# A decoder layer on one core: the first 128 tokens go ahead through attention output, output projection and queries, and VectorE weights three of the last v rows

## The reference

```python
y_a = a_pre @ w_conv_out
y_b = attn_o @ w_attn_out
mix = jax.nn.sigmoid(g_a) * y_a + jax.nn.sigmoid(g_b) * y_b
x = x + gate1[:, None, :] * (mix @ w_out)
h2 = _modulate(_rmsnorm(x, norm2_w), shift2, scale2)
y = _peer(h2.reshape(-1, D_MODEL), peer_w_q, peer_sub_keys, peer_u, peer_v).reshape(x.shape)
return x + gate2[:, None, :] * y
```

```python
act = jax.nn.gelu(jnp.einsum('thkd,td->thk', u_tab[e], hb).astype(jnp.float32))
return jnp.einsum('thk,thkd->td', (g * act).astype(hb.dtype), v_tab[e])
```

## Time and profile before

| | us |
|---|---|
| median of 3 runs (1149.05 to 1152.76) | 1151.59 |
| the profiled execution | 1151.69 |
| its span, first to last instruction | 1149.9 |
| TensorE busy | 983.1 |
| VectorE busy | 718.0 |
| POOL busy (asking) | 575.2 |
| ScalarE busy | 242.6 |

### The profile page before, as it was taken

The page is one execution under the profiler, slowest core; times in us unless marked ns, Lnnn a source line. Parts: engine busy times, 40 slices in busy tenths (PEclk is TensorE's granted clock), DMA queues, the critical chain, the costliest instruction groups (busy, mean ns, idle before and its releaser), DMA issues.

```text
span 1149.9 us, 10850 instructions
## 1 busy us (share of the span) xinstructions
PE 983.1 (85%) x3401; PEld 497.9 (43%) x3401; DVE 718.0 (62%) x1765; ACT 242.6 (21%) x593; POOL 575.2 (50%) x618
## 2 busy tenths in 40 slices
PE   6998889999999999998777777777777777778888
PEld 3456766667677874542232222222222222222333
DVE  2357466888644798768567467477576576444342
ACT  2111223113402133341112112121121021121111
POOL 0201001002000567777777777777777777777760
PEclk9999889999999999999999999999999999999999
DMA  9961423779537699999999999999999999999994
GB/s 314 351 221 57 152 74 129 256 256 286 148 120 287 245 345 382 409 408 410 409 409 409 409 410 409 409 409 410 410 409 409 410 409 410 409 410 409 409 411 179
DMA packets 123403, 379.89 MB, mean 330 GB/s; under 512 B 11612, under 2 KB 21080, under 8 KB 123348
## 3 DMA queue, kind: packets, MB, share of 16 engines
q0 software_dynamic: 86208, 312.92, 69.3%
q1 hardware_dynamic: 36966, 66.19, 16.7%
q10 hardware_dynamic: 174, 0.11, 0.1%
HBM read 377.59 MB, written 1.59 MB: 330 GB/s over the span
## 4 chain that ended last, share of the span: by engine, by line
PE 37%; DMA 28%; POOL 20%; issue 8%; DVE 6%; ACT 1%; SPq 0%; DVEq 0%; ACTq 0%; POOLq 0%
DMA big<-peer_v,oT 13%; POOL big L1060 9%; POOL big L1049 8%; PE twoA L567 7%; DMA big<-peer_u,oT 7%; PE twoA L880 5%; DMA r<-peer_u,oT 4%; PE twoD L935 4%; PE twoD L937 3%; PE twoD L821 3%; PE twoA L545 2%; POOL r L1049 2%; PE twoA L490 2%; PE twoD L809 1%; DMA big<-w_in 1%
## 5 line engine op out<-in xcount | busy, mean ns | idle before, releaser
L1049 POOL DMA_INDIRECT big<-peer_u,oT x230 | 216.5, 941 | 179.1 <-DVEq L1777 107.0
L1060 POOL DMA_INDIRECT big<-peer_v,oT x266 | 252.6, 950 | 87.5 <-issue 69.6
L1819 DVE CUSTOM_DVE_ANT_0 big<-big,twoA 128x1024 f32<-128x1024 f32 x128 | 156.2, 1221 | 143.5 <-DMA big<-peer_u,oT 142.5
L1819 DVE CUSTOM_DVE_ANT_0 big<-big,twoD 128x1024 f32<-128x1024 f32 x102 | 123.3, 1218 | 54.9 <-DMA big<-peer_u,oT 53.6
L935 PE MATMUL twoD<-big 128*128 128x512 f32 x176 | 97.0, 633 | 40.4 <-DMA big<-peer_v,oT 38.7
L567 PE MATMUL twoA<-hT,big 128*128 128x288 f32 x448 | 117.6, 419 | 0.0
L935 PE MATMUL twoD<-big,modT 128*128 128x512 f32 x132 | 73.1, 636 | 31.1 <-DMA big<-peer_v,oT 30.7
L567 PEld LDWEIGHTS twoA<-hT,big 128*128 128x128 f32 x448 | 86.2, 196 | 28.8 <-issue 5.9
L937 PE MATMUL twoD<-big 128*128 128x512 f32 x176 | 89.9, 592 | 0.0
L935 PEld LDWEIGHTS twoD<-big 128*128 128x128 f32 x176 | 27.5, 188 | 104.6 <-DMA big<-peer_v,oT 96.4
L935 PE MATMUL twoD<-big,rstd 128*128 128x512 f32 x90 | 49.9, 636 | 21.8 <-DMA big<-peer_v,oT 21.7
(11 more groups left out here) (368 smaller groups left out, 1419.0 us busy)
## 6 DMA issues: line engine op xcount, KB each, us to landing
big<-w_ada SPq DMA_DIRECT2D x12, 2048.0 KB, 8.3
big<-w_in SPq DMA_DIRECT2D x5, 2048.0 KB, 13.6
big<-w_in SPq DMA_DIRECT2D x9, 1024.0 KB, 7.6
big<-peer_w_q SPq DMA_DIRECT2D x3, 2048.0 KB, 8.8
big<-peer_v,oT POOLq DMA_INDIRECT x266, 18.5
big<-w_out SPq DMA_DIRECT2D x2, 2048.0 KB, 11.7
big<-peer_u,oT POOLq DMA_INDIRECT x230, 16.3
big<-w_conv_out SPq DMA_DIRECT2D x1, 2048.0 KB, 13.7
```

The source lines that it names most:

```text
L1049: pool.indirect_dma_start(urows[i % NU], None, peer_u, bass.IndirectOffsetOnAxis(ap=eidx[:, t, s:s + 1], axis=0)).then_inc(u_in[i % NU], 16)
L1060: pool.indirect_dma_start(vrows[j % NV], None, peer_v, bass.IndirectOffsetOnAxis(ap=eidx[:, t, s:s + 1], axis=0)).then_inc(v_in[j % NV], 16)
L1819: dve.tensor_tensor_reduce(out=urows[i % NU], in0=urows[i % NU], in1=h2tok[t][:, :], scale=1.0, scalar=0.0, op0=ALU.mult, op1=ALU.add, acc ...
```

## The change

`attnout`, `out`, residual, norm and the first eight query blocks are done in two passes: columns 0 to 127 (tile 0, whose attention is long finished) and columns 128 to 287 (REST, 160 wide).

- First pass: `attnout` in two packs of 16 matmuls, before and after the turned probabilities; `out` right behind the sample values. w_out's first half moves to slot 1, free after conv out; the first query weights to slot 6. The sigmoid is taken in four pieces between the copies of the last turned keys. Head 0 and head 1 of tile 0 are scored before the second pass starts.
- Second pass: on two other banks (R), three groups of blocks (RESTS). VectorE mixes them before the first dot, does the three residuals after dots 3, 6 and 8 (REST_AT) and the norm after dot 12 (REST_NORM). Query blocks 4 to 7 for tile 0 lie in front of it.
- The remaining query blocks alternate with the first 24 products, by the table SLOTS_BY. The leftover work starts at slot 26, not 6.
- Buffers: 6 u rows until slot 30, then 10; 4 v rows until slot 16, 9 until slot 34, then 13, since their places still hold weights. The lag begins at 14, reaches 20, and shrinks to 8.
- v rows of slots 281, 283 and 285 are weighted and added by VectorE into one row, scaled by the gate, and summed over the four partitions by two more matmuls.

Cut to what moves:

```diff
-        LAG, NEAR, LAST_NEAR = 18, 8, 4
+        LAG, NEAR, LAST_NEAR = 20, 14, 8
+        U_FIRST, U_ROWS = 30, 6
+        V_FIRST, V_ROWS, V_SOME = 16, 4, 34
...
+        BY_VECTOR = (281, 283, 285)
+        REMAIN = sum(SLOTS) - len(BY_VECTOR)
...
-                ("out", cols(w_out, 0, 512), 5), ("out", cols(w_out, 512, 512), 6),
-                ("peerq", peer_cols(0), 5), ("peerq", peer_cols(1), 4), ("peerq", peer_cols(2), 0), ("peerq", peer_cols(3), 1)]
+                ("out", cols(w_out, 0, 512), 1), ("out", cols(w_out, 512, 512), 5),
+                ("peerq", peer_cols(0), 6), ("peerq", peer_cols(1), 4), ("peerq", peer_cols(2), 0), ("peerq", peer_cols(3), 1)]
...
-        LATE = list(range(6, 6 + 2 * 15, 2))
...
-        SCORE_AFTER = [4, 8, 12]
-        EARLY = {8: 0, 12: 1}
+        REST_AT, REST_NORM = (3, 6, 8), 12
+        RESTS = ((0, 3), (3, 6), (6, DC))
+        SLOTS_BY = [2 + j for j in range(8)] + [10 + 2 * j for j in range(8)]
+        SCORE_AFTER = {11: 3, 15: 4}
+        QUERIES = {0: 2, 1: 4, 2: 8, 3: 20}
+        EARLY_EXP, EARLY_GELU = {1: 1}, {1: 1, 6: 2, 9: 3, 11: 4, 15: 5}
+        u_row = [i % U_ROWS if i < U_FIRST else (i - U_FIRST + U_ROWS) % NU for i in range(ROUNDS)]
+        v_some = (4, 0, 1, 2, 3, 5, 6, 7, 8)
+        v_all = (9, 10, 11, 12) + v_some
+        v_row = [j % V_ROWS if j < V_FIRST else v_some[(j - V_FIRST) % 9] if j < V_SOME else v_all[(j - V_SOME) % NV]
+                 for j in range(ROUNDS)]
...
+            def attn_first(i):
+
+                if i == 0:
+                    pe.wait_ge(oT_ready, 1)
+                    slot[0] = weights(pe, group("attnout"))
+                b = V.open(pe)
+                for j in range(4):
+                    for k in range(4):
+                        mm = pe.matmul(b[:, j * P:(j + 1) * P], slot[0][:, k, (4 * i + j) * P:(4 * i + j + 1) * P], oT[:, k, 0:P],
+                                       start=(k == 0), stop=(k == 3))
+                V.close(mm)
+
+            def out_first(j):
+
+                w = weights(pe, group("out", j // 4))
+                b = V.open(pe)
+                for k in range(DC):
+                    if j == 0:
+                        pe.wait_ge(mix_ready, k // 4 + 1)
+                    mm = pe.matmul(b[:, 0:P], w[:, k, (j % 4) * P:(j % 4 + 1) * P], mixT[:, k, 0:P], start=(k == 0), stop=(k == DC - 1))
+                V.close(mm)
+                if j >= 2:
+                    square_sum(j - 2, 1)
...
             sample_scores(0)
             sample_scores(1)
             conv_out(CONV_FILL[1])
             conv_held.append((bankA[(A.n - 1) % 4], A.n))
+            attn_first(0)
             turn_probs(0)
             turn_probs(1)
+            attn_first(1)
             sample_values(0)
             sample_values(1)
+            pe.wait_ge(a_free, A.n)
+            sum_bank.append(bankA[(A.n + 3) % 4])
+            for j in range(4):
+                out_first(j)
...
-            pe.wait_ge(oT_ready, 3)
-            g = group("attnout")
-            w = weights(pe, g)
-            for j in range(DC):
-                b = V.open(pe)
-                for k in range(4):
-                    mm = pe.matmul(b[:, 0:TOK], w[:, k, j * P:(j + 1) * P], oT[:, k, 0:TOK], start=(k == 0), stop=(k == 3))
-                V.close(mm)
...
+            for j in range(4, DC):
+                out_first(j)
...
-                pe.wait_ge(qp_ready, 2 if n == 0 else 2 + 2 * (h + nh))
+                pe.wait_ge(qp_ready, QUERIES.get(n, 24))
...
+            pair = [A.open(pe) for _ in range(2)]
+            for k in range(DC):
+                pe.wait_ge(h_ready, DC + k + 1)
+                for j in range(2):
+                    mm = pe.matmul(pair[j][:, 0:P], first[:, k, j * P:(j + 1) * P], hT[:, k, 0:P], start=(k == 0), stop=(k == DC - 1))
+            A.close(mm, 2)
             pe.wait_ge(d_free, V.n)
             turn_h2(0)
             score_unit(0)
...
+            for j in (2, 3):
+                query(j, 0, P)
+            score_unit(1)
+
+            pe.wait_ge(oT_ready, 3)
+            w = weights(pe, group("attnout"))
+            for a, e in RESTS:
+                b = R.open(pe)
+                for j in range(a, e):
+                    for k in range(4):
+                        mm = pe.matmul(b[:, (j - a) * REST:(j - a + 1) * REST], w[:, k, j * P:(j + 1) * P], oT[:, k, P:TOK],
+                                       start=(k == 0), stop=(k == 3))
+                R.close(mm)
+            released[group("attnout")] = (r_full, R.n)
+            for n, (a, e) in enumerate(RESTS):
+                b = R.open(pe)
+                for j in range(a, e):
+                    g = group("out", j // 4)
                     w = weights(pe, g)
-                b, begin = A.open(pe), P if j < 2 else 0
-                for k in range(DC):
-                    if j == 0:
-                        pe.wait_ge(h_rest, k + 1)
-                    mm = pe.matmul(b[:, begin:TOK], w[:, k, (j % 4) * P:(j % 4 + 1) * P], hT[:, k, begin:TOK], start=(k == 0),
-                                   stop=(k == DC - 1))
-                A.close(mm)
-                released[g] = (a_full, A.n)
-                if j in SCORE_AFTER:
-                    score_unit(SCORE_AFTER.index(j) + 1)
-            score_unit(4)
+                    for k in range(DC):
+                        if j == 0:
+                            pe.wait_ge(mix_ready, 3 if k < 3 else 4 if k < 6 else 5)
+                        mm = pe.matmul(b[:, (j - a) * REST:(j - a + 1) * REST], w[:, k, (j % 4) * P:(j % 4 + 1) * P], mixT[:, k, P:TOK],
+                                       start=(k == 0), stop=(k == DC - 1))
+                    released[g] = (r_full, R.n)
+                R.close(mm)
+            for j in (4, 5):
+                query(j, 0, P)
+            b = A.open(pe)
+            pe.wait_ge(sq_ready, 2 * DC + 3)
+            for c in range(DC):
+                mm = pe.matmul(b[:, 0:REST], ones[:, :], sqR[:, c, :], start=(c == 0), stop=(c == DC - 1))
+            A.close(mm)
+            rest_sum.append((a_full, A.n))
+            for j in (6, 7):
+                query(j, 0, P)
+            score_unit(2)
+            pe.wait_ge(r_free, R.n)
...
+            multiplied = 0
+            for j in range(16):
+                while multiplied < SLOTS_BY[j]:
+                    products(multiplied)
+                    multiplied += 1
+                if j == 0:
+                    pe.wait_ge(h_ready, 2 * DC + 1)
+                query(j, P if j < 8 else 0, TOK, ready=(j == 0))
+                if j in SCORE_AFTER:
+                    score_unit(SCORE_AFTER[j])
+            for j in range(multiplied, ROUNDS):
+                if j not in BY_VECTOR:
+                    products(j)
+            pe.wait_ge(part_scaled, 1)
+            for half in range(2):
+                pe.matmul(bankD[2 + half][0:NSM, :], cv["sum4"], vrows[v_row[BY_VECTOR[0]]][:, half * 512:(half + 1) * 512],
...
-                if g == group("out"):
+                if g == group("out", 1):
...
+                before = row_before(u_row, i)
+                if before is not None:
+                    pool.wait_ge(u_used, before + 1)
+                elif u_row[i] >= U_ROWS:
                     pool.wait_ge(*released[group("peerq")])
...
+                before = row_before(v_row, j)
+                if before is not None:
+                    pool.wait_ge(v_used, before + 1)
+                elif v_row[j] < 4:
+                    pool.wait_ge(*released[group("out", 1)])
                 else:
-                    pool.wait_ge(v_used, j - NV + 1)
-                pool.indirect_dma_start(vrows[j % NV], None, peer_v,
-                                        bass.IndirectOffsetOnAxis(ap=eidx[:, t, s:s + 1], axis=0)).then_inc(v_in[j % NV], 16)
-
-            pool.wait_ge(*released[group("out", 1)])
+                    pool.wait_ge(*released[group("peerq", 1 if v_row[j] == 4 else 2 if v_row[j] < 9 else 3)])
...
-                lag = min(LAG, NEAR + 4 + i // 4, LAST_NEAR + (ROUNDS - 1 - i) // 2)
+                lag = min(LAG, NEAR + i // 6, LAST_NEAR + (ROUNDS - 1 - i) // 2)
...
+                part = sig[:, 4 * (bb - KB):4 * (bb - KB) + 4, :].rearrange("p j t -> p (j t)")
+                L.tell(act.activation(part, part, ACT.Sigmoid), gates_ready)
...
+            made = 0
+            for j in range(16):
+                while made < SLOTS_BY[j]:
+                    diagonal(made)
+                    made += 1
+                copy_query(j, P if j < 8 else 0, TOK)
+                if j in EARLY_EXP:
+                    exps(EARLY_EXP[j])
+                if j in EARLY_GELU:
+                    gelus(EARLY_GELU[j])
+                if j in SCORE_AFTER:
+                    copy_scores()
+            for j in range(made, ROUNDS):
+                diagonal(j)
...
+            def mix(b, j, n, a, e):
+
```

(19 more changed lines are left out.)

237 lines of the change are left out of this document (129 added, 108 removed).

## The result

The changed kernel takes **1175.8 us** (median of 4, 1174.95 to 1176.24), the kernel before 1152.0 beside it (1149.05 to 1152.76): a ratio of 1.0211, 95% interval 1.0194 to 1.0229. It is 24 us slower; the forecast was 1142, 10 us faster. The profiled span is 1173.2 us against 1149.9. Executions that the chip's slower state had disturbed are left out (two, both of e2: 1407 and 3411 us).

A forecast was written before the change was run, and what follows sets the result against it. The gathers of u and v rows at 409.5 GB/s were taken to bound the kernel. From 1151.7, less 7.2 (ramp), plus 1.0 (thin queue), less 4.0 (tail) gave 1141.5, say 1142 us; range 1133 to 1152.

The forecast's parts named there:

- the sum: TensorE's ramp from its first product: 24 products, 16 query blocks and 2 scorings take 90.9 us, product 24 at 489.8.

The follow-up runs named there:

- e2: The changed kernel with two query blocks between two or four products instead of one block between one or two: 1174.45 and 1175.84 us.
- b3: The kernel before with only the distance of the last u and v rows at 8 slots instead of 4: 1155.3 us; first run 1234.6 against 1230.8.
- h2: Changed kernel, diagonals a turn ahead, u rows 28 ahead, earlier gelus, later weighing and routing, old end (distance 4, no VectorE slots): 1141.2 us; first run 1218.5.

## What to carry to other kernels

Where two engines alternate, sum the ring, not the busy time of one: write down for each turn which instruction of engine B stands ahead of the one that engine A waits for, and make it a turn earlier. Where one queue asks for two kinds of rows in order, the slower kind sets the pace of both, and an earlier start is only a loan that is called in at the first place where the other kind is short. A parameter that is changed together with a saving (a distance, a lag) is costed by itself, since it can take exactly what the saving brings.

## What was not expected of the hardware

TensorE's granted clock fell to 1.2 GHz in the new ramp. In the kernel after it was 0.56 from 386 to 392 and 0.50 from 400 to 404, after stretches in which TensorE had been busy about half the time (4.7 of 10 us, 4.3 of 8):

```profile
376.00:386.00 10.00, 4.74 (x41) 4.55 (x39) 9.52 (x34) 0.60 (x1) 3.01 (x4) 0.93 1.03 398
386.00:392.00 6.00, 4.85 (x21) 4.88 (x22) 5.53 (x13) 1.37 (x4) 3.17 (x4) 0.56 0.90 323
392.00:400.00 8.00, 4.34 (x37) 3.96 (x35) 7.68 (x18) 6.26 (x16) 5.80 (x7) 0.88 0.91 306
400.00:404.00 4.00, 3.41 (x4) 1.51 (x5) 4.00 (x22) 0.74 (x3) 2.80 (x3) 0.50 0.97 324
```

A pair of product matmuls takes 2.05 us there and 1.02 later. The kernel before kept 1.00 from 376 to 424, with TensorE busy throughout on its query blocks. In the kernel after the clock was low once more, 0.79 from 416 to 424, behind the gap of 3.9 us. The two places cost some 4 us (first two products 5.7 us instead of 3.4, the third turn's product and block 5.8 instead of 4.1), about half of the 8.7 us by which the chain's busy time exceeds the sum.

One chip (first runs of b3 and h2) granted a mean clock of 0.85 to 0.90 from 600 to 1150 us, and the gathers moved 370 to 374 GB/s where every other profiled run had 1.00 and 409; the kernel before took 1230.8 us on it. Whether the clock or the queues came first can't be told from these runs.
